# Four gates of the second branch made inside the delta rule of the last layer, and kept in the free half of the merge's sum buffer

## The chip, the cores and the metric

The kernel runs on one core of a Trainium2 chip. A core has five engines that run apart and meet through semaphores: TensorE (PE, matmuls into eight banks of PSUM; PEld is its weight load), VectorE (DVE), ScalarE (ACT), GpSimd (POOL) and SyncE (SP), which here only issues weight transfers. The metric is device time in microseconds of one launch. Everything is float32.

## The reference, cut to what matters

Two layers; each token stream has 256 context and 256 latent tokens (512 columns in all), and the model width is 1024.

```
px = in_projection(rmsnorm(x) * (1 + scale) + shift, w_in)
oa = bidirectional chunked gated linear attention        (branch 0, GLA)
ob = bidirectional chunked gated delta rule, conv'd q/k/v (branch 1, GDN)
oc = multi-head latent attention                          (branch 2, MLA)
y_i = head_norm(o_i) * silu(z_i)
ys  = y_i @ w_branch[i]                # per branch, 1024 x 1024
gates = sigmoid(px['merge_gate'])      # 3 branches x 1024 channels
x  = x + gate_x * (sum_i gates_i * ys_i) @ w_out
```

The second layer updates only the latent stream, so its merge works on 256 columns (LC to T) of each buffer, and the first 256 columns are free there.

## The kernel before, in words

**A list of items sets every engine's order.** `schedule()` writes one list of items, such as `("gate", l, br, e)`: layer `l`, branch `br`, block `e` of 128 output channels. Each engine's program walks that one list, so what is moved in it is moved on all engines at once. `weave` mixes several lists evenly by their load; `settle` then shifts some kinds by a fixed number of places. `pieces` cuts a long matmul item in four: a gate, or a `ys` product, is four pieces of two matmuls with 256 columns each, and the trace holds every such float32 matmul as two records. Banks and the four slots of the weight ring (`ring`, 1 MB a transfer) are dealt out in the order of this list.

**A gate.** PE makes the logits of 128 channels (8 matmuls). ACT takes absolute value, exp and ln(1+x) into one of two buffers `E1`, DVE a minimum and a subtraction (`("v", "gate", ...)`), and ACT's last exp gives the sigmoid. Normally that last exp belongs to the item `ys`; then DVE multiplies it by the product of `ys` and adds it into `MT`, the merge's sum buffer.

**Kept gates.** Six gates of branch 2 in the last layer are made early: `kept_gates` puts them into the delta rule, and an item `gx` writes their last exp into the context half of `yT`, where DVE's `ys` reads them.

**The delta rule of the last layer** (`gdn`) has four rounds `g`, two heads each. `head` prepares a round (`d1`, `d2`, `dd`, `dt`); `sol` solves the small triangular systems on POOL, with transfers before and after; `invert` (`dv` first, then `dx`, `dya`, `dyb`, `dx6`, `dy6`) puts the inverses together on PE, DVE and ACT; the scan (`st`, `su`, `sk`, `sq`, `sa`) follows. While POOL solves round g+1, PE projects q, k and v (`dqkv`) and scans round g. The list `fill` is spread over the rounds in shares 1, 1, 1, 2: first the kept gates, then the merge of branch 0 (8 gates and 8 `ys`).

**Latent attention** (`mla`) follows: low-rank projections (`mkv`, `mq`), the projections up (`muk`, `muq`, `mkT`, `mqT`), then scores, softmax and output (`ms`, `mp`, `mo`) in four rounds. Its first part is woven with the gate path of branch 1: `z` (matmul), `("v","z")` (DVE), `z2` (ACT exp, then three DVE operations, L1872, L1874, L1879) and `yT` (PE transposes, L1087, and a DVE copy, L1890). The rest is woven with the merge of branch 1, `m`. Its first `lead` items stand ahead of `rest`, mixed with the last transposes.

The lines that the prediction names: L1084 and L1087 the matmuls and the transposes, L1437 to L1439 ACT's three operations of a gate or a `z`, L1617 ACT's last exp, L1854 DVE's step on a `z`, L2104 the four DVE copies of `dv`, L2055 DVE's end of `dn`.

Of the kernel before, what the change touches and what calls it, by code (L numbers as in the profile page):

```python
# [9 lines left out]
ACT = mybir.ActivationFunctionType  # L10
# [7 lines left out]
DEPTH = 2  # L18
LC = LX = 256
T = LC + LX  # L20
# [100 lines left out]
    return NB // 2 - 1 - n if n < NB // 2 else 3 * NB // 2 - 1 - n  # L121


def keeps(it):

    return it[0] in ("gate", "ys") and it[1] == DEPTH - 1 and it[2] == 2 and it[3] < 6


def ahead(it):
# [24 lines left out]
def pieces(it):  # L154

    return [("pc",) + it + (i,) for i in range(NPIECE[it[0]] - 1)] + [it]
# [16 lines left out]
def schedule():  # L173
# [18 lines left out]
    def yts(l, br):  # L192
        return [("yT", l, br, tt, 1) for tt in tiles(l)]

    def kept_gates(l):

        out = []
        for e in range(6):
            out += pieces(("gate", l, 2, e)) + [("v", "gate", l, 2, e), ("gx", l, 2, e)]
        return out  # L200

    def merge(l, br):
        if keeps(("gate", l, br, 0)):
            out = [i for e in range(6, 8) for i in pieces(("gate", l, br, e)) + [("v", "gate", l, br, e)]]
            return out + [i for e in range(8) for i in pieces(("ys", l, br, e))]
        out = []
        for e in range(9):
            if e < 8:
                out += pieces(("gate", l, br, e))
            p = pieces(("ys", l, br, e - 1)) if e else []  # L210
            out += p[:2] + ([("v", "gate", l, br, e)] if e < 8 else []) + p[2:]
        return out

    def mods(todo):
# [144 lines left out]
    for l in range(DEPTH):  # L359
        s += [("nx", l)] * (l > 0) + [("nh", l)]  # L360
        s += gla(l)
        s += [("rstd", l, 0)]
        fill = merge(l, 0)
        if keeps(("gate", l, 2, 0)):
            fill = kept_gates(l) + fill
        s += gdn(l, zs(l, 0) + yts(l, 0), fill)
        s += [("rstd", l, 1)]
        first, rest = mla(l)
        lead = len(pieces(("gate", l, 1, 0))) + 1
        m = merge(l, 1)  # L370
        z = zs(l, 1)
        s += z[:5] + weave(first, z[5:] + weave(yts(l, 1), m[:lead]))
        s += weave(rest, m[lead:])
        m = merge(l, 2)
        lead = 5 * (8 - 6) if keeps(("gate", l, 2, 0)) else lead
        s += zs(l, 2) + weave(yts(l, 2), m[:lead]) + m[lead:]
        sums = pieces(("norm", l + 1)) if l < DEPTH - 1 else []
        for e in range(8):
            s += [("out", l, e)] + sums[e - 2:e - 1] * (e >= 2)
        if sums:  # L380
            s += sums[6:7] + [("mod", l + 1, 4)] + sums[7:] + [("modT", l + 1, 4), ("mod", l + 1, 5), ("modT", l + 1, 5)]
# [74 lines left out]
def hybrid_block(nc, x, c, ctx_in, c_ctx, norm_w, ada_w, ada_b, w_in, gla_gate_w2, gla_gate_b, gla_norm_w,  # L456
# [20 lines left out]
    for now, it in enumerate(plan):  # L477
        it = it[1:-1] if it[0] == "pc" else it
# [31 lines left out]
    with ExitStack() as stack:  # L510
# [5 lines left out]
        MT = sb("MT", [P, KT, T])  # L516
        yT = sb("yT", [P, KT, T])
# [15 lines left out]
        E1 = sb("E1", [P, 2, 512])  # L533
# [394 lines left out]
        zg_index = {i: n for n, i in enumerate(zg)}  # L928
# [503 lines left out]
        def _(act):  # L1432
# [43 lines left out]
            for it in plan:  # L1476
                k, l = it[0], it[1]
                if k == "nh":
                    act.wait_ge(*done(("modT", l, 5 if l else 3), "dve"))
                    act.wait_ge(s_scw, l + 1)  # L1480
                    for kk in range(KT):
# [3 lines left out]
                        for s in range(2):  # L1485
                            sel = 1 - s
                            ins = nc.scalar.activation(seg(hT[:, kk, :], s), seg(hT[:, kk, :], s), ACT.Identity,
                                                       bias=MOD[:, l, kk, sel:sel + 1], scale=SCW[:, kk, sel:sel + 1])
# [10 lines left out]
                if k == "xin":  # L1499
                    _, tt, h = it  # L1500
                    ins = nc.scalar.activation(yT[:, 4 * h:4 * h + 4, tt * P:(tt + 1) * P],
                                               ps[:, :].rearrange("p (j n) -> p j n", j=4), ACT.Copy)
                elif k == "xout":
                    _, tt, h = it
                    ins = nc.scalar.activation(O[:, tt, h * 512:(h + 1) * 512], ps[:, :], ACT.Copy)  # L1505
                elif k == "par":
# [4 lines left out]
                    ins = nc.scalar.activation(SCt[:, 0, :], PAR[:, l, PR_C:PR_C + 16], ACT.Exp, scale=-1.0) if l == 0 else \  # L1511
                        nc.scalar.activation(SCt[:, 1, 0:1], EPSC[:, :], ACT.Copy)
                elif k == "norm":
# [11 lines left out]
                    ins = rsqrt(RS[:, :], ps[:, :], D)  # L1525
                elif k == "lr":
                    ins = nc.scalar.activation(LRT[0:LROW, :], ps[0:LROW, :], ACT.Copy)
                elif k == "gqk":
                    _, l, g, j = it
                    a0 = q0 if j < 2 else 0  # L1530
                    ins = nc.scalar.activation(QK[:, g, j, a0:T], ps[:, a0:T], ACT.Copy)
                elif k == "gv":
                    _, l, g, tt = it
                    ins = nc.scalar.activation(V[:, g, tt, :], ps[:, :], ACT.Copy)
                elif k == "ga":
                    p = prev_kind(it)
                    if p:
                        act.wait_ge(*done(p, "dve"))
                    p = plan_prev(it, ("go",))
# [3 lines left out]
                    ins = log1p_exp(LT1, ps[:, :])  # L1543
                elif k == "gb":
                    p = prev_kind(it)
# [4 lines left out]
                    ins = nc.scalar.activation(EI, ps[:, :], ACT.Exp, scale=-1.0 / 16)  # L1550
                elif k == "ge":
                    p = prev_kind(it)
# [4 lines left out]
                    ins = nc.scalar.activation(AER, ps[:, :], ACT.Exp, scale=1.0 / 16)  # L1557
                elif k == "gw":
                    _, l, h, r, n = it
# [4 lines left out]
                    ins = nc.scalar.activation(HQ[:, r, n, :], HS[:, r, :], ACT.Copy, scale=AMID[:, r, at:at + 1])  # L1564
                elif k == "go":
                    _, l, h, tt = it
                    act.wait_ge(*done(plan_prev(it, ("go", "ga")), "act"))
                    if plan_prev(it, ("go", "ga"))[0] == "ga":
                        act.wait_ge(*done(plan_prev(it, ("ga",)), "dve"))
                    ins = nc.scalar.activation(LT1[:, 0:ADV], ps[:, 0:ADV], ACT.Square,  # L1570
                                               accum_out=SSQ[:, 0, tt, h:h + 1])
                elif k == "osq":
                    _, l, g, p = it
# [7 lines left out]
                    for i in range(4):  # L1581
                        tt, h = 2 * p + i // 2, 2 * g + i % 2
                        ins = nc.scalar.activation(RS[:, i * P:(i + 1) * P], O[:, tt, h * P:(h + 1) * P], ACT.Square,
                                                   accum_out=SSQ[:, 1, tt, h:h + 1])
                elif k == "rstd":
                    _, l, br = it
# [8 lines left out]
                    ins = rsqrt(SSQ[:, br, t0:TT, 0:nh], SSQ[:, br, t0:TT, 0:nh], hd)  # L1595
                elif k in ("z", "gate"):
                    n = zg_index[it]
                    if n >= 2:
                        p = zg[n - 2]
# [5 lines left out]
                    ins = log1p_exp(E1[:, n % 2, a0:512], ps[:, a0:512])  # L1605
                elif k == "gx":
                    gi = ("gate",) + it[1:]
                    act.wait_ge(*done(gi, "dve"))
                    act.wait_ge(s_spill, 16 * (l + 1))
                    act.wait_ge(s_scaled, KT * (l + 1))  # L1610
                    ins = nc.scalar.activation(yT[:, it[3], 0:LC], E1[:, zg_index[gi] % 2, LC:T], ACT.Exp)
                elif k in ("z2", "ys"):

                    zi = ("z" if k == "z2" else "gate",) + it[1:]
# [1 line left out]
                    e = E1[:, zg_index[zi] % 2, (q0 if k == "ys" else 0):512]  # L1616
                    ins = nc.scalar.activation(e, e, ACT.Exp)  # L1617
                elif k == "dg":
# [14 lines left out]
                    ins = nc.scalar.activation(ERV[:, :, :], ERV[:, :, :], ACT.Exp)  # L1633
                elif k == "dqkv":
                    act.wait_ge(s_zero, 4 * l + 3)
                    pj = dq_index[it] % 2
                    p = prev_kind(it, 2)
                    if p:
                        act.wait_ge(*done(("cv",) + p[1:] + (CONV - 1,), "dve"))
                    a0 = 1 if (it[3] < 2 and l == DEPTH - 1) else 0  # L1640
                    ins = nc.scalar.activation(PAD[:, 2 * pj + a0:2 * pj + 2, 2:258],  # L1641
                                               ps[:, a0 * LC:T].rearrange("p (s n) -> p s n", n=LC), ACT.Copy)
                elif k == "dsilu":
                    act.wait_ge(*done(("cv",) + it[1:] + (CONV - 1,), "dve"))
                    p = prev_kind(it)
# [4 lines left out]
                    ins = log1p_exp(CE[:, a0:T], CA[:, pj, a0:T])  # L1650
# [130 lines left out]
        def _(dve):  # L1781
            entered = set()
            V_ = nc.vector
            for it in plan:
# [113 lines left out]
                elif k == "ys":  # L1898
# [2 lines left out]
                    e = E1[:, zg_index[gi] % 2, q0:512]  # L1901
                    if keeps(it):
                        dve.wait_ge(*done(("gx",) + it[1:], "act"))
                        e = yT[:, e8, 0:LC]
                    else:
                        dve.wait_ge(*done(it, "act"))
                    m = MT[:, e8, q0:T]
# [380 lines left out]
```

## Time and profile before

| | us |
|---|---|
| median of 3 runs | 2272.14 (2269.09 to 2276.57) |
| the profiled execution | 2264.7 |
| its span | 2262.9 |
| mean granted TensorE clock | 0.979 |
| PE busy | 2144.7 (95%) |
| DVE, ACT, POOL busy | 929.3, 845.4, 363.9 |

The second layer's delta rule lies between about 1573 and 1940 us of the span, its latent attention between about 1941 and 2169. "busy" of PE counts modelled ends of pipelined matmuls; the true price of a matmul is read from the distance of its records' starts. The granted clock is given as a share of 2.4 GHz; it is either 1 or 0.5 at any time.

### The profile page before, as it was taken

What the parts mean: (1) busy time and instruction counts of PE and PEld (TensorE: products, weight loads), DVE (VectorE), ACT (ScalarE), POOL (GpSimd) and SP (SyncE); (2) the same over time, 40 slices, a digit from 0 to 9 for tenths busy, and PEclk for the clock granted to TensorE, in tenths of its full rate; (3) what the DMA queues carried; (4) which work ended last, traced back from release to release, by engine and by line L of the source; (5) the groups of instructions that cost most, each with busy time, mean ns of one, the idle gap of its engine ahead of it and who ended that gap; (6) DMA issues with size and microseconds to landing.
All of it is one profiled execution on the core that took longest, in us unless ns stands there. A gap on an engine that the chain in (4) does not pass through costs nothing. (4 is left out here: it accounts for less than half of the span.)

```text
span 2262.9 us, 31475 instructions
## 1 busy us (share of the span) xinstructions
PE 2144.7 (95%) x10970; PEld 1464.3 (65%) x10970; DVE 929.3 (41%) x2271; ACT 845.4 (37%) x2205; POOL 363.9 (16%) x591
## 2 busy tenths in 40 slices
PE   6999899999989999999999999999989978999998
PEld 3667576655555786555674446777576657877687
DVE  2023374757563325433331120236566653343321
ACT  2123263536443224444331112246455443244420
POOL 1000007071542000000000010000734752000000
PEclk8999999999999999999999999999999999999999
DMA  8224412211212022111222333121322222332333
GB/s 287 70 75 142 141 41 63 87 50 53 84 29 66 29 65 87 58 42 44 75 75 74 112 116 113 59 76 40 119 76 69 65 71 69 100 104 74 120 123 120
DMA packets 191420, 190.16 MB, mean 84 GB/s; under 512 B 28559, under 2 KB 185955, under 8 KB 190755
## 3 DMA queue, kind: packets, MB, share of 16 engines
q1 hardware_dynamic: 186048, 171.08, 23.9%
q0 software_dynamic: 3648, 16.72, 2.3%
q8 instruction: 93, 1.52, 0.3%
q10 hardware_dynamic: 1571, 0.34, 0.1%
q14 instruction: 60, 0.49, 0.1%
HBM read 178.62 MB, written 9.50 MB: 83 GB/s over the span
## 5 line engine op out<-in xcount | busy, mean ns | idle before, releaser
L1084 PE MATMUL bank<-hT,ring 128*128 128x512 f32 (+2 forms) x1856 | 718.8, 535 | 3.0 <-DVE hT L1845 1.5
L1084 PEld LDWEIGHTS bank<-hT,ring 128*128 128x128 f32 (+1 forms) x1856 | 332.6, 190 | 257.5 <-issue 240.0
L1084 PE MATMUL bank<-ring,hT 128*128 128x256 f32 (+2 forms) x2112 | 454.2, 370 | 11.6 <-DMA ring<-in_w_in_dram 11.6
L1084 PE MATMUL bank<-WORK 128*128 128x128 f32 (+6 forms) x3056 | 392.9, 287 | 42.0 <-DVE O L2104 17.7
L1084 PEld LDWEIGHTS bank<-ring,hT 128*128 128x128 f32 x2112 | 383.4, 192 | 75.2 <-issue 28.4
L1084 PEld LDWEIGHTS bank<-WORK 128*128 128x128 f32 (+4 forms) x3056 | 322.0, 171 | 145.9 <-issue 123.8
L1084 PE MATMUL bank<-yT,ring 128*128 128x512 f32 (+1 forms) x768 | 272.0, 492 | 0.0
L1084 PEld LDWEIGHTS bank<-yT,ring 128*128 128x128 f32 x768 | 140.4, 192 | 84.5 <-issue 76.0
L1048 POOL TENSOR_TENSOR WORK<-WORK 64x31 f32<-64x31 f32 (+15 forms) x248 | 152.0, 613 | 19.4
L2031 DVE SCALAR_TENSOR_TENSOR WORK<-WORK,CW 128x512 f32<-128x512 f32 (+1 forms) x192 | 147.1, 766 | 2.3
L1046 POOL TENSOR_TENSOR WORK<-WORK 64x31 f32<-64x31 f32 (+15 forms) x248 | 142.3, 574 | 19.5
L1437 ACT ACTIVATE E<-bank 128x512 f32<-128x512 f32 (+1 forms) x84 | 44.9, 535 | 253.5 <-PE bank L1084 253.3
L1072 POOL DMA_DIRECT2D yT<-xs x2 | 1.1, 536 | 808.0 <-DVE MT L1915 808.0
L1084 PE MATMUL bank<-ring,WORK 128*128 128x384 f32 (+1 forms) x272 | 108.4, 536 | 0.0
L1449 ACT ACTIVATE WORK<-bank 128x128 f32<-128x128 f32 (+3 forms) x182 | 47.2, 271 | 133.0 <-PE bank L1084 133.0
L1084 PE MATMUL bank<-MT,ring 128*128 128x512 f32 (+1 forms) x256 | 83.8, 486 | 2.7 <-DVE MT L1915 2.7
L1087 PEld LDWEIGHTS bank<-K,WORK 128*128 128x128 f32 (+1 forms) x506 | 64.9, 145 | 31.5 <-issue 23.8
L1087 PE MATMUL bank<-K,WORK 128*128 128x128 f32 (+1 forms) x506 | 82.9, 282 | 0.0
L1084 PEld LDWEIGHTS bank<-ring,WORK 128*128 128x128 f32 x272 | 50.3, 190 | 37.9 <-issue 22.0
L1084 PEld LDWEIGHTS bank<-MT,ring 128*128 128x128 f32 x256 | 48.5, 190 | 37.2 <-issue 30.1
L1933 DVE SCALAR_TENSOR_TENSOR WORK<-bank,WORK 128x512 f32<-128x512 f32 x16 | 11.1, 692 | 139.2 <-ACT WORK L1439 139.2
L1641 ACT ACTIVATE WORK<-bank 128x512 f32<-128x512 f32 (+1 forms) x48 | 26.8, 559 | 98.1 <-PE bank L1084 98.1
(205 smaller groups left out, 2085.1 us busy)
## 6 DMA issues: line engine op xcount, KB each, us to landing
ring<-in_w_in_dram SPq DMA_DIRECT2D x92, 1024.0 KB, 5.2
ring<-in_ada_w_dram SPq DMA_DIRECT2D x24, 1024.0 KB, 6.0
ring<-in_w_branch_dram SPq DMA_DIRECT2D x24, 1024.0 KB, 5.1
ring<-in_w_out_dram SPq DMA_DIRECT2D x8, 1024.0 KB, 5.0
ring<-in_mla_q_up_dram SPq DMA_DIRECT2D x8, 576.0 KB, 4.6
xs<-yT POOLq DMA_DIRECT2D x2, 2048.0 KB, 10.6
ring<-in_mla_kv_up_dram SPq DMA_DIRECT2D x8, 512.0 KB, 3.7
yT<-xs POOLq DMA_DIRECT2D x2, 2048.0 KB, 9.1
```

Source lines behind the costliest of these rows:

```text
L1046: link(pool, "pool", pool.tensor_tensor(t, a[:, j + 1:BASE, j:j + 1].broadcast_to([q, m, w]), y[:, j:j + 1, 0:w].broadcast_to([q, m, w]), ...
L1048: ins = pool.tensor_tensor(y[:, j + 1:BASE, 0:w], y[:, j + 1:BASE, 0:w], t, ALU.subtract)
L1072: pool.dma_start(yT[:, :, :], xs[l]).then_inc(s_back, 16)
L1084: return nc.tensor.matmul(o, a, b, start=start, stop=stop, skip_group_check=True)
L1087: return nc.tensor.transpose(o, a, ident)
L1437: link(act, "act", nc.scalar.activation(dst, src, ACT.Abs))
L1449: ins = nc.scalar.activation(MT2[:, c0:c0 + w], ps[:, c0:c0 + w], ACT.Square, accum_out=mS[:, at + i:at + i + 1])
L1641: ins = nc.scalar.activation(PAD[:, 2 * pj + a0:2 * pj + 2, 2:258], ps[:, a0 * LC:T].rearrange("p (s n) -> p s n", n=LC), ACT.Copy)
L1933: ins = V_.scalar_tensor_tensor(LA[:, tt, :], ps[:, :], 0.0, LT1, ALU.min, ALU.subtract)
L2031: ins = V_.scalar_tensor_tensor(acc, src, wv, acc, ALU.mult, ALU.add)
```

## The change

`KEPT` now holds how many gates of each branch are kept: none of branch 0, four of branch 1, six (as before) of branch 2. The four new ones are made in the delta rule behind the six, and are written into the context half of `MT`. The merge of branch 1 loses their pieces and the DVE step; and the number of items that lead it goes from five (one gate) to none.

```diff
+KEPT = (0, 4, 6)
+
+
 def keeps(it):
 
-    return it[0] in ("gate", "ys") and it[1] == DEPTH - 1 and it[2] == 2 and it[3] < 6
+    return it[0] in ("gate", "ys") and it[1] == DEPTH - 1 and it[3] < KEPT[it[2]]
...
         for e in range(9):
             if e < 8:
-                out += pieces(("gate", l, br, e))
+                out += [] if keeps(("gate", l, br, e)) else pieces(("gate", l, br, e))
             p = pieces(("ys", l, br, e - 1)) if e else []
-            out += p[:2] + ([("v", "gate", l, br, e)] if e < 8 else []) + p[2:]
+            out += p[:2] + ([("v", "gate", l, br, e)] if e < 8 and not keeps(("gate", l, br, e)) else []) + p[2:]
...
         if keeps(("gate", l, 2, 0)):
-            fill = kept_gates(l) + fill
+            fill = kept_gates(l, 2) + kept_gates(l, 1) + fill
         s += gdn(l, zs(l, 0) + yts(l, 0), fill)
         s += [("rstd", l, 1)]
         first, rest = mla(l)
-        lead = len(pieces(("gate", l, 1, 0))) + 1
+        lead = 0 if keeps(("gate", l, 1, 0)) else len(pieces(("gate", l, 1, 0))) + 1
         m = merge(l, 1)
         z = zs(l, 1)
         s += z[:5] + weave(first, z[5:] + weave(yts(l, 1), m[:lead]))
         s += weave(rest, m[lead:])
...
-                    ins = nc.scalar.activation(yT[:, it[3], 0:LC], E1[:, zg_index[gi] % 2, LC:T], ACT.Exp)
+                    ins = nc.scalar.activation((yT if it[2] == 2 else MT)[:, it[3], 0:LC], E1[:, zg_index[gi] % 2, LC:T], ACT.Exp)
...
-                        e = yT[:, e8, 0:LC]
+                        e = (yT if br == 2 else MT)[:, e8, 0:LC]
```

TensorE, the scan of the last round of the delta rule, from the first `st` on. `WORK x4` is a step of the scan, `hT,ring` are gate pieces and `yT,ring` pieces of `ys` of branch 0 (x2 is one piece). Before:

```order
L1084 MATMUL bank2<-WORK 128x128 x4
L1084 MATMUL bank5<-hT,ring 128x256 x2
L1084 MATMUL bank3<-WORK 128x128 x4
L1084 MATMUL bank5<-hT,ring 128x256 x2
L1084 MATMUL bank0<-WORK 128x128 x4
L1084 MATMUL bank5<-hT,ring 128x256 x2
L1084 MATMUL bank1<-yT,ring 128x256 x2
L1084 MATMUL bank7<-WORK 128x128 x4
L1084 MATMUL bank1<-yT,ring 128x256 x2
L1084 MATMUL bank6<-WORK 128x128 x4
```

And now (all lines of the program stand three further down):

```order
L1087 MATMUL bank4<-WORK 128x128 x4
L1087 MATMUL bank3<-yT,ring 128x256 x2
L1087 MATMUL bank2<-WORK 128x128 x4
L1087 MATMUL bank3<-yT,ring 128x256 x4
L1087 MATMUL bank7<-WORK 128x128 x4
L1087 MATMUL bank0<-hT,ring 128x256 x4
L1087 MATMUL bank6<-WORK 128x128 x4
L1087 MATMUL bank0<-hT,ring 128x256 x2
L1087 MATMUL bank5<-WORK 128x128 x4
L1087 MATMUL bank0<-hT,ring 128x256 x2
```

Between the same steps of the scan stand one or two pieces where there was one.

TensorE, where latent attention goes from its first part to the scores, from the second `muq` on. `ring,WORK` are `muq` and `muk`, `K,O x4` is a `yT`, `K,WORK` a transpose of keys (x2) or queries (x3), `hT,ring` a gate piece. Before:

```order
L1084 MATMUL bank5<-ring,WORK 128x384 x3
L1084 MATMUL bank3<-ring,WORK 128x512 x2
L1084 MATMUL bank0<-hT,ring 128x256 x2
L1087 MATMUL bank7<-K,WORK 128x128 x2
L1087 MATMUL bank4<-K,O 128x128 x4
L1087 MATMUL bank6<-K,WORK 128x128 x2
L1084 MATMUL bank2<-ring,WORK 128x512 x2
L1084 MATMUL bank0<-hT,ring 128x256 x2
L1087 MATMUL bank5<-K,WORK 128x128 x2
L1084 MATMUL bank0<-hT,ring 128x256 x2
L1087 MATMUL bank3<-K,WORK 128x128 x3
L1087 MATMUL bank1<-K,O 128x128 x4
```

And now:

```order
L1087 MATMUL bank3<-ring,WORK 128x384 x3
L1087 MATMUL bank1<-ring,WORK 128x512 x2
L1090 MATMUL bank7<-K,O 128x128 x4
L1090 MATMUL bank4<-K,WORK 128x128 x2
L1087 MATMUL bank2<-ring,WORK 128x512 x2
L1090 MATMUL bank6<-K,WORK 128x128 x2
L1090 MATMUL bank3<-K,WORK 128x128 x2
L1090 MATMUL bank1<-K,O 128x128 x4
L1090 MATMUL bank7<-K,WORK 128x128 x3
L1090 MATMUL bank4<-K,O 128x128 x4
L1090 MATMUL bank2<-K,WORK 128x128 x2
L1090 MATMUL bank0<-K,O 128x128 x4
```

The gate pieces are gone from here, and all four `yT` now stand behind the last `z`, close to each other (one stood ahead of the first `muq` before).

VectorE at the same place: L1854 (L1857 now) is the step on the last `z`, L1872 to L1879 (L1875 to L1882) a `z2`, L1890 (L1893) the copy of a `yT`. Before:

```order
L1854 SCALAR_TENSOR_TENSOR E1<-bank1,E1 128x512
L1872 TENSOR_TENSOR E1<-E1,bank4 128x512
L1874 TENSOR_TENSOR O<-O,SSQ 128x512
L1879 TENSOR_TENSOR O<-O,E1 128x512
L2216 TENSOR_TENSOR WORK<-bank6,WORK 128x256
L1890 TENSOR_TENSOR yT<-bank2,NW4 128x4x128
```

And now, from the last `muk` (L2219) on:

```order
L2219 TENSOR_TENSOR WORK<-bank2,WORK 128x256
L1875 TENSOR_TENSOR E1<-E1,bank0 128x512
L1877 TENSOR_TENSOR O<-O,SSQ 128x512
L1882 TENSOR_TENSOR O<-O,E1 128x512
L1857 SCALAR_TENSOR_TENSOR E1<-bank5,E1 128x512
L1893 TENSOR_TENSOR yT<-bank1,NW4 128x4x128
L2239 TENSOR_SCALAR WORK<-bank7,QKW 128x2x128
L1875 TENSOR_TENSOR E1<-E1,bank5 128x512
L1877 TENSOR_TENSOR O<-O,SSQ 128x512
L1882 TENSOR_TENSOR O<-O,E1 128x512
```

Both last `z2` now stand behind the last `muk`, close together; before, thirteen other instructions stood between the two, and the first was ahead of the last `muk`.

## Rows read from the trace of the kernel before

**Rows 1.** The page: the kernel's engines, busy time and share.

```profile
PE 2144.7 (95%) x10970; PEld 1464.3 (65%) x10970; DVE 929.3 (41%) x2271; ACT 845.4 (37%) x2205; POOL 363.9 (16%) x591
```

**Rows 2.** Busy time by stretch, last layer; first the stretch and its length.

```profile
core 0: us, PE busy (x) PEld busy (x) DVE busy (x) ACT busy (x) POOL busy (x), PEclk, DMA share, GB/s
1584.60:1651.00 66.40, 55.92 (x200) 35.51 (x198) 37.52 (x61) 25.22 (x48) 45.40 (x69) 0.96 0.41 125
1673.20:1736.00 62.80, 61.56 (x279) 41.64 (x277) 41.69 (x86) 31.23 (x70) 43.14 (x69) 1.00 0.32 95
1736.00:1756.70 20.70, 18.20 (x302) 16.25 (x301) 15.86 (x45) 16.01 (x43) 0.00 (x0) 0.92 0.09 21
1756.70:1816.00 59.30, 57.19 (x253) 38.37 (x252) 39.95 (x78) 28.04 (x63) 43.33 (x69) 1.00 0.24 69
1816.00:1831.30 15.30, 11.66 (x80) 10.33 (x79) 11.26 (x32) 9.82 (x26) 0.00 (x0) 1.00 0.52 149
1831.30:1889.20 57.90, 40.82 (x432) 34.65 (x432) 25.62 (x67) 19.94 (x52) 40.72 (x69) 0.90 0.18 53
1889.20:1940.00 50.80, 50.17 (x476) 43.51 (x477) 18.61 (x53) 16.71 (x45) 0.08 (x1) 0.94 0.26 84
2024.50:2169.00 144.50, 144.50 (x673) 103.13 (x672) 50.98 (x168) 66.19 (x252) 0.00 (x0) 1.00 0.26 85
```

**Rows 3.** Busy time by stretch, three with the half clock.

```profile
1649.40:1656.10 6.70, 4.37 (x82) 3.79 (x84) 5.95 (x19) 2.30 (x5) 0.00 (x0) 0.50 0.01 2
1833.70:1843.80 10.10, 5.33 (x44) 4.24 (x44) 2.35 (x6) 4.08 (x11) 6.61 (x13) 0.50 0.07 27
1888.30:1895.10 6.80, 5.84 (x84) 4.51 (x85) 2.21 (x8) 5.78 (x16) 0.00 (x0) 0.50 0.01 2
```

**Rows 4.** The chain that ended last, around 1885 us: start, length, what.

```profile
1883.85 4.25 DMA WORK<-XD
...
1889.26 3.13 PE bank L1084 x62
```

**Rows 5.** The same chain, behind latent attention.

```profile
2190.81 3.46 PE bank L1084 x16
...
2225.12 27.88 PE bank L1084 x128
```

**Rows 6.** TensorE in order of time, in brackets the idle time before.

```profile
1651.73 0.55 PE L1084 MATMUL bank<-WORK 128*128 128x128 f32 x1 [5.74 <-DVE WORK L2055]
...
1889.26 0.23 PE L1084 MATMUL bank<-WORK 32*32 32x32 f32 x1 [6.22 <-DVE O L2104]
```

**Rows 7.** Groups of TensorE by shape, 2024.5 to 2169 us: the gates' pieces.

```profile
L1084 PE MATMUL bank<-hT,ring 128*128 128x256 f32 x112 | 28.9, 382 | 0.0
```

**Rows 8.** VectorE in order of time, around the first of the last two `z2`.

```profile
2013.69 0.68 DVE L1854 SCALAR_TENSOR_TENSOR E<-bank,E 128x512 f32<-128x512 f32 x1
2014.29 0.68 DVE L1872 TENSOR_TENSOR E<-E,bank 128x512 f32<-128x512 f32 x1
...
2015.60 0.69 DVE L1879 TENSOR_TENSOR O<-O,E 128x512 f32<-128x512 f32 x1
...
2020.88 0.69 DVE L1879 TENSOR_TENSOR O<-O,E 128x512 f32<-128x512 f32 x1
2021.49 0.68 DVE L1890 TENSOR_TENSOR yT<-bank,NW 128x512 f32<-128x512 f32 x1
2022.09 0.41 DVE L2216 TENSOR_TENSOR WORK<-bank,WORK 128x256 f32<-128x256 f32 x1
```

**Rows 9.** ScalarE: the last exp of a `z2`, and its first and last operation of a `muk`.

```profile
2018.40 0.61 ACT L1617 ACTIVATE E<-E 128x512 f32<-128x512 f32 x1
...
2020.34 0.38 ACT L1742 ACTIVATE WORK<-bank 128x256 f32<-128x256 f32 x1 [0.78 <-PE bank L1084]
...
2021.60 0.20 ACT L1459 ACTIVATE WORK<-WORK 128x2 f32<-128x2 f32 x1
```

**Rows 10.** TensorE from the first to the last transposes of branch 1.

```profile
2006.78 0.60 PE L1087 MATMUL bank<-K,O 128*128 128x128 f32 x4
...
2022.41 0.60 PE L1087 MATMUL bank<-K,O 128*128 128x128 f32 x4
2022.85 0.38 PE L1087 MATMUL bank<-K,WORK 128*128 128x128 f32 x2
```

More of the change, by code:

```diff
@@ L193, in yts, with kept_gates @@
         return [("yT", l, br, tt, 1) for tt in tiles(l)]
-    def kept_gates(l):
+    def kept_gates(l, br):
         out = []
-        for e in range(6):
-            out += pieces(("gate", l, 2, e)) + [("v", "gate", l, 2, e), ("gx", l, 2, e)]
+        for e in range(KEPT[br]):
+            out += pieces(("gate", l, br, e)) + [("v", "gate", l, br, e), ("gx", l, br, e)]
         return out
     def merge(l, br):
-        if keeps(("gate", l, br, 0)):
+        if br == 2 and keeps(("gate", l, br, 0)):
             out = [i for e in range(6, 8) for i in pieces(("gate", l, br, e)) + [("v", "gate", l, br, e)]]
@@ L374, in schedule @@
         m = merge(l, 2)
-        lead = 5 * (8 - 6) if keeps(("gate", l, 2, 0)) else lead
+        lead = 5 * (8 - 6) if keeps(("gate", l, 2, 0)) else len(pieces(("gate", l, 2, 0))) + 1
         s += zs(l, 2) + weave(yts(l, 2), m[:lead]) + m[lead:]
```

## The prediction

> **What bounds the kernel now.** First the page: PE is busy 95% of the span and no other engine over 41% [rows 1]. So what counts is PE's time, and the question is only where PE still waits. I read that from the busy time by stretch [rows 2], in which the last layer's delta rule is cut where its rounds hand over. Three kinds of stretch are seen.
>
> PE-bound ones: 1673.2 to 1736.0 and 1756.7 to 1816.0, the POOL solves of rounds 1 and 2 (counted from 0). PE is busy 61.56 of 62.80 and 57.19 of 59.30 us [rows 2], although POOL works beside it. Latent attention from 2024.5 to 2169 is busy for all of its 144.50 us [rows 2].
>
> One that waits for POOL: 1831.3 to 1889.2, the solve of round 3. PE is busy only 40.82 of 57.90 us, so it idles 17.1 us [rows 2]. The chain runs through POOL and its transfer, and PE starts only behind it [rows 4], after a last wait of 6.22 us for DVE's `dv` [rows 6].
>
> Short ones bound by DVE, ACT and PE in turn: 1736.0 to 1756.7 and 1816.0 to 1831.3. Then 1889.2 to 1940, round 3's inversion and scan, with PE busy for 50.17 of 50.80 us [rows 2].
>
> **The price of a piece.** Eight matmuls with 256 columns are 16 records; 3.46 us of the chain hold 16 of them [rows 5]. A piece is two matmuls, so 0.865 us. The end of the chain confirms it: 64 matmuls in 27.88 us are 0.871 us for two [rows 5]. Four gates are sixteen pieces, 13.8 us of PE, which leave latent attention and enter the delta rule. (The mean of 382 ns a record [rows 7] can't be used for this: the records overlap.)
>
> **Where the pieces arrive.** I counted gate and `ys` pieces of the last layer in the list before and after, between the marks of the stretches:
> - up to the start of round 1's solve: 4 and 4;
> - from there to round 1's `dx`: 12 and 15, so 3 more, 2.6 us, where PE is the bound;
> - in round 1's inversion: 3 and 3;
> - from the start of round 2's solve to that of round 3: 15 and 18, 3 more, 2.6 us, PE-bound but for its last 15 us, which get no more than they had;
> - from the start of round 3's solve to its `dx`: 22 and 24, 2 more, 1.7 us, in the stretch with 17.1 us of idle PE. They cost nothing as long as POOL is late; without this cover they would cost 1.7 us;
> - from round 3's `dx` to the end of the delta rule: 32 and 40, 8 more, 6.9 us.
>
> The sum is 16. Fourteen stand where PE has no room: 12.1 us. Three of the last eight stand in round 3's inversion, a chain over DVE and ACT as well, and one `dqkv` piece moves into round 1's inversion, where PE waits; I take 1.1 us off: **+11.0 us**, between +8 (all that is woven into inversions and scan stalls hidden, for which 0.6 us of idle PE behind 1889.2 [rows 2] speaks poorly) and +13.8.
>
> The other work of the four gates is small: three ACT operations and a `gx`, one DVE operation. It leaves attention and enters the delta rule, where ACT is busy 31.23 of 62.80 us and DVE 41.69 [rows 2]; both are below PE, and the new steps stand beside steps of the same kind. 0, at most +2 us, if some of them delays a piece of the scan. The two weight transfers move along; each has tens of us of other work between the release of its slot and its first use.
>
> **What latent attention gives back.** Twelve of the sixteen pieces stand between the scores' start and the end: 10.4 us. It is busy throughout, with no idle time before it [rows 2, 7], so I count them in full, less 1.0 us for a few short distances (keys' projection to transposition, scores to softmax) which lose a piece: **-9.4 us**.
>
> The other four were `lead`, 3.5 us among the last transposes. Here I expect the change to lose. Before, PE had 15.6 us of work between the first and the last `yT` [rows 10], and the last one came without a wait: DVE's last `z2` had ended at 2020.88 + 0.69 = 2021.57 and PE began at 2022.41 [rows 8, 10]. In the new order both last `z2` stand behind the last `muk` on DVE. From the end of that `muk` on PE the chain is: ACT's part, 2020.34 to 2021.80, 1.46 us; its exp 0.61 [rows 9]; a `z2`, from 2014.29 to 2015.60 + 0.69, 2.0 us; the step on the last `z` 0.6; the copy of a `yT` 0.6; the queries' scaling 0.4; the other `z2` 2.0 [rows 8]. Sum 7.6 us. PE has in that time two transposes of keys, one of queries, two `yT` and one more of keys; a `yT` of four transposes takes 0.44 us [rows 10], the whole 1.9 us. So it waits some 5.7 us, in two waits around the third `yT`. Against the 3.5 us of pieces that are gone, this place ends 2 us later than before: **+2.0 us**, between -3.5 (no wait) and +4.
>
> Then the clock. Behind waits of 5.74 and 6.22 us [rows 6] PE's granted clock is 0.50 for 6.7 and 6.8 us [rows 3], the 1.2 GHz level. I expect the same here, for 3.4 to 6.8 us, and PE at half speed loses half of it: **+2.4 us**, from 0 to +3.4. The half clock around 1838 and 1888 [rows 3] lies in or behind POOL's stretch as before.
>
> **The sum.** 11.0 - 9.4 + 2.0 + 2.4 = +6.0 us on the profiled execution's 2264.7, so 2270.7. Its time is 7.4 below the median of the runs shown, 2272.1; on that footing the forecast is **2278 us**. About 0.3%, 6.8 us, is what a measurement of this kernel can tell from no change, so +6.0 is just inside.
>
> **The rivals.**
>
> Faster: the delta rule has idle PE, and the pieces fill it. For it: 17.1 us idle in one stretch alone and 3.6 more in 1816 to 1831 [rows 2]. Were all sixteen covered and no new wait made, the time would fall by 9.4 + 3.5 = 12.9 us; with half of them covered and the wait at the entry, nothing would be gained. Against it: the shares of `fill` put two of sixteen pieces into that stretch. Its mechanism would be that POOL paces rounds 1 and 2 too, so that their six pieces are free (-5.2), that half of the last eight go into hidden stalls (-3.4), and that the entry to attention ends where it did (0 for 2.0 and 2.4): 2.4 - 9.4 = -7.0 us, 2265.
>
> Neutral: the counts are right but the entry to attention does not wait, as DVE and ACT have less to do there than I take. Then 11.0 - 9.4 - 3.5 = -1.9 us, 2270. For it: before, the same steps ended 0.8 us early [rows 8, 10].
>
> Slower by more: attention is not bound by PE's matmuls, and gives back only a part. It decides from the point where PE, with fewer pieces, has to wait for the softmax (ACT is busy 66.19 of 144.50 us there [rows 2]). With half of the 9.4 us lost: +10.7, 2283. Against it: PE is busy without a gap [rows 2], and 0.865 us apiece is the distance of starts and not a modelled end [rows 5].
> The Trainium skill bears on this one, in "Perfetto Trace Analysis", section "Identifying the Most-Contended Engine": a busy share of matmuls is a poor measure of PE's headroom, and the share of the weight loads is to be read. That share is 103.13 of 144.50 us here, 71%. By this rule a third of the stretch would be headroom, and an estimate by it lets the twelve pieces give back some two thirds, 6.3 us, which makes +9.1 in all.
>
> That the change doesn't do what it says is excluded by the order: the gates stand in the delta rule, and attention has 48 gate and `ys` pieces left of 64.
>
> **How the numbers follow.** Forecast 0.58, neutral 0.16, faster 0.09, slower by more 0.17. The forecast's own uncertainty is about 4 us each way, so of its 0.58 I put 0.33 within 0.3% and 0.25 above it. The neutral case lies within, the slower one above; of the faster one 0.07 is under -0.3%. Together faster 0.07, same 0.51, slower 0.42. The range of 8 in 10 leaves out a tenth on each side: from 2266 (the faster case's edge) to 2286 (the slower one with POOL's cover gone as well).
>
> **What would show it.** Right: the starts of round 2's and round 3's solves 2.6 and 5.2 us later; PE's idle time between round 3's solve and its `dx` smaller by about 2 us; round 3's `dx` to the end of the delta rule longer by about 7; a wait of PE before an L1090 transpose for DVE's L1882, 5 to 6 us, where there was none, and the half clock behind it; from the scores' start to the end of attention about 9 us less. Wrong: solves that start at most 1 us later (faster), no such wait (neutral), or new waits of PE in the scores and softmax (slower).

## The result, and the profile after

| | before | after |
|---|---|---|
| median, us | 2271.07 (4 runs, 2269.09 to 2276.57) | 2287.28 (4 runs, 2284.50 to 2290.88) |
| profiled execution | 2264.7 | 2288.93 |
| its span | 2262.9 | 2287.1 |
| mean granted TensorE clock | 0.979 | 0.972 |

The ratio is 1.0068, 95% interval [1.0044, 1.0092]: 15.4 us slower, where +6.0 was forecast. The time lies 1.3 us above the range.

The two profiled executions must not be subtracted whole. Up to the last layer's first `d1`, where both kernels issue the same work, they already differ by 9.4 us (1563.6 and 1573.0). From that `d1` to the end of the last output's product it is 689.4 us before and 704.3 after, unrounded **+14.8 us**, close to the timed +15.4. So every difference below is one of lengths, each taken between two events of one execution.

The page's engines, answering to [rows 1]. PE's busy time is no less than before, in a longer span.

```profile
PE 2155.1 (94%) x10970; PEld 1470.1 (64%) x10970; DVE 930.5 (41%) x2271; ACT 845.3 (37%) x2205; POOL 361.4 (16%) x591
```

Busy time by stretch of after, answering to [rows 2, 3]: start and end, length, then busy time (records) of PE, PEld, DVE, ACT, POOL, the granted clock, the share of the DMA engines and their GB/s.

```profile
1594.00:1660.40 66.40, 55.70 (x200) 35.41 (x198) 37.36 (x61) 25.22 (x48) 45.35 (x69) 0.96 0.42 125
1682.60:1745.40 62.80, 61.09 (x276) 41.53 (x276) 42.53 (x85) 30.58 (x68) 42.74 (x69) 1.00 0.32 93
1767.00:1829.60 62.60, 61.14 (x276) 42.11 (x275) 40.00 (x81) 31.19 (x69) 42.49 (x69) 1.00 0.29 86
1829.60:1844.90 15.30, 11.59 (x69) 10.25 (x67) 10.99 (x30) 8.09 (x23) 0.00 (x0) 0.89 0.34 100
1844.90:1904.90 60.00, 42.82 (x444) 36.56 (x444) 24.81 (x66) 22.21 (x58) 40.90 (x69) 0.88 0.26 78
1904.90:1960.00 55.10, 54.99 (x501) 48.54 (x502) 18.98 (x54) 17.68 (x44) 0.00 (x0) 0.95 0.25 78
1897.20:1910.90 13.70, 5.91 (x88) 4.72 (x89) 2.62 (x9) 5.86 (x16) 1.20 (x1) 0.50 0.18 55
2047.40:2054.20 6.80, 5.56 (x13) 2.95 (x15) 2.35 (x4) 0.00 (x0) 0.00 (x0) 0.50 0.00 0
2020.00:2055.10 35.10, 29.55 (x113) 18.68 (x112) 17.25 (x43) 16.75 (x68) 0.00 (x0) 0.90 0.38 124
2055.10:2192.90 137.80, 132.40 (x615) 93.02 (x616) 49.31 (x162) 60.15 (x236) 0.00 (x0) 1.00 0.25 78
```

The row to 1960.00 ends with the last `sa`. Before, the last `sa` ends at 1938.5, so the row to 1940.00 of [rows 2] is 1.5 us longer than that stretch, and the lengths to compare are 49.3 and 55.1 us.

The last two rows are the entry to latent attention and the rest of it. The mark between them is the end of the first pair of scores: PE issues the scores of two heads together, and the last matmuls of both stand in the second one's item, so that neither can be used earlier. The entry runs from the end of the last `mq` to this mark, the rest from the mark to the end of the last `mo`; below they are called "ahead of" and "behind the first scores". The same two stretches of before:

```profile
1999.40:2027.20 27.80, 27.80 (x121) 18.76 (x120) 17.23 (x44) 16.38 (x69) 0.00 (x0) 1.00 0.56 174
2027.20:2168.70 141.50, 141.50 (x664) 102.13 (x664) 50.26 (x165) 65.17 (x248) 0.00 (x0) 1.00 0.27 87
```

Here is the point that the forecast missed. Behind the first scores PE is busy for 141.50 - 132.40 = 9.1 us less, about what was expected (9.4). But the stretch is only 3.7 us shorter: 5.4 us have turned into idle time. PE in order of time, with the idle time before each group in brackets; the first row answers to the last of [rows 6]:

```profile
1904.99 0.23 PE L1087 MATMUL bank<-WORK 32*32 32x32 f32 x1 [11.77 <-DVE O L2107]
...
2045.12 0.63 PE L1090 MATMUL bank<-K,O 128*128 128x128 f32 x4 [2.58 <-DVE O L1882]
...
2048.64 1.09 PE L1090 MATMUL bank<-K,O 128*128 128x128 f32 x4 [2.67 <-DVE O L1882]
...
2057.88 2.58 PE L1087 MATMUL bank<-WORK 128*128 128x512 f32 x6 [1.77 <-DVE WORK L2239]
...
2089.26 0.41 PE L1090 MATMUL bank<-K,WORK 128*128 128x128 f32 x2 [0.75 <-DVE WORK L2219]
...
2096.49 1.10 PE L1087 MATMUL bank<-WORK 128*128 128x512 f32 x2 [1.79 <-DVE WORK L2239]
```

The two waits for L1882 are the forecast ones. Those for L2239, the scaling of queries (`mqT`), were not foreseen. What stands before it on ACT and DVE, after:

```profile
2055.13 0.69 DVE L2249 TENSOR_REDUCE WORK<-bank 128x1 f32<-128x512 f32 x1 [4.68 <-PE bank L1087]
2055.86 0.15 DVE L2250 TENSOR_SCALAR WORK<-WORK 128x1 f32<-128x1 f32 x1
2056.09 0.69 ACT L1769 ACTIVATE WORK<-bank,WORK 128x512 f32<-128x512 f32 x1 [9.58 <-PE bank L1087]
2056.68 0.19 ACT L1769 ACTIVATION_READ_ACCUMULATOR WORK<-bank,WORK 128x1 f32 x1
2056.77 0.27 ACT L1760 ACTIVATE WORK<-bank 128x128 f32<-128x128 f32 x1
2057.15 0.48 DVE L2239 TENSOR_SCALAR WORK<-bank,QKW 128x256 f32<-128x256 f32 x1 [1.14 <-ACT WORK L1760]
```

The first score's maximum (L2249, L2250) and its exp (L1769) stand ahead of the copy (L1760) and the scaling (L2239) of the round's last queries, each on its engine. The maximum itself had waited 4.68 us for the end of the first pair. So the scores of the last 128 queries wait for the softmax of the first score. Before, the scaling came first and the maximum second, and PE did not wait:

```profile
2025.68 0.48 DVE L2236 TENSOR_SCALAR WORK<-bank,QKW 128x256 f32<-128x256 f32 x1 [1.60 <-ACT WORK L1757]
...
2027.28 0.69 DVE L2246 TENSOR_REDUCE WORK<-bank 128x1 f32<-128x512 f32 x1 [1.11 <-PE bank L1084]
```

The reason is in `settle`: it moves each `ms` two places earlier, whatever stands there. Before, in the list ahead of this shift, one item of the merge lay between the last `mqT` of each round and its first `ms` (DVE's step of gate 0 in round 0, a piece of gate 3, 5 or 7 in the others). With gates 0 to 3 gone nothing lies there in rounds 0 and 1, and the `ms` passes the `mqT`; in rounds 2 and 3 a piece of a `ys` product still lies there, and there is no such wait.

### The profile page after: what moved, and what is told of

Read it like the earlier page. It is cut to its first block and busy times, and to the rows that moved or that the text cites. A ratio compares the mean times of both kernels' runs of the same rounds, so it can differ in the third digit from the quotient of the medians.

```text
span 2287.1 us, 31483 instructions
## 1 busy us (share of the span) xinstructions
PE 2155.1 (94%) x10970; PEld 1470.1 (64%) x10970; DVE 930.5 (41%) x2271; ACT 845.3 (37%) x2205; POOL 361.4 (16%) x591
## 5 line engine op out<-in xcount | busy, mean ns | idle before, releaser
L1087 PE MATMUL bank<-WORK 128*128 128x128 f32 (+6 forms) x3056 | 400.1, 290 | 50.7 <-DVE O L2107 24.2
L1087 PEld LDWEIGHTS bank<-WORK 128*128 128x128 f32 (+4 forms) x3056 | 326.6, 174 | 156.5 <-issue 133.6
L1936 DVE SCALAR_TENSOR_TENSOR WORK<-bank,WORK 128x512 f32<-128x512 f32 x16 | 11.1, 692 | 140.1 <-ACT WORK L1442 140.1
## 6 DMA issues: line engine op xcount, KB each, us to landing
xs<-yT POOLq DMA_DIRECT2D x2, 2048.0 KB, 11.2
```

Of the source, the lines that this page charges most:

```text
L1087: return nc.tensor.matmul(o, a, b, start=start, stop=stop, skip_group_check=True)
L1936: ins = V_.scalar_tensor_tensor(LA[:, tt, :], ps[:, :], 0.0, LT1, ALU.min, ALU.subtract)
```

## The experiments

The letters A to D are those of the expectations; B and D mean something else in each run and are defined there. A is the account above: a piece costs 0.865 us where PE has no room and nothing where PE waits for POOL, and waits come from fixed shifts in a list that has become shorter. C is the prediction's rival "slower by more": attention isn't bound by PE. Each change in microseconds is the ratio times 2271. "The region" is again from the last layer's first `d1` to the last output's product, minus the 689.4 us of before. It comes from one execution of each kernel, and the time from several. In the edits, `...` marks what is left out.

**e1: the attention half alone.** The four gates are made nowhere (`ys` reads what the sum buffer holds), and the merge of branch 1 is as in after.

```diff
-            fill = kept_gates(l, 2) + kept_gates(l, 1) + fill
+            fill = kept_gates(l, 2) + fill
...
```

(The lines left out let DVE's `ys` go on without waiting for a gate.)

> The attention half of the change alone: the four gates of branch 1 are left out altogether (neither made in the delta rule nor in attention; its sums use what stands in the buffer), so 13.8 us of TensorE are gone from attention and nothing is added. Theory A (the trace of after: from the end of the delta rule to the end of the kernel it is 2.7 us longer than before, for all its missing pieces; the two waits at the entry, 2.6 and 2.7 us, and two of 1.8 us in which a score waits for the queries' scaling, take back the gain): before +1 to +4 us. Theory B (the attention gives back what the prediction said, -9.4 +2.0 +2.4 = -5, and the rest of the loss is made in the delta rule): before -5 us or less.

Measured: 2274.02 (12 runs), ratio 1.0012 [1.0003, 1.0022], +2.7 us; region +1.7. Taking 13.8 us of matmuls away makes the kernel no faster. The waits are those of after, in PE's order of time:

```profile
2028.51 0.63 PE L1090 MATMUL bank<-K,O 128*128 128x128 f32 x4 [2.64 <-DVE O L1882]
2032.02 1.09 PE L1090 MATMUL bank<-K,O 128*128 128x128 f32 x4 [2.67 <-DVE O L1882]
2041.04 3.01 PE L1087 MATMUL bank<-WORK 128*128 128x512 f32 x8 [1.76 <-DVE WORK L2240]
```

**e2: the delta-rule half alone.** Four extra gates are made in the delta rule and read by nobody; attention keeps its own.

```diff
-        for e in range(KEPT[br]):
+        for e in range(6) if br == 2 else range(8, 12):
...
```

(The lines left out keep gates 0 to 3 in attention and say where the extra ones are written.)

> The delta rule's half alone: four gates more are made in the delta rule of the last layer (of other channels, written to the free half of the sum buffer and not read), and attention keeps all of its gates and its order. Two more weight transfers in all. Theory A (fourteen of sixteen pieces stand where TensorE has no room; the trace of after is 12.1 us longer there): before +11 to +13 us. Theory B (the delta rule loses more than TensorE's price, by ScalarE and the weight ring): before +17 us or more. If the idle time of the solves took the pieces up, it would be +3 us or less.

Measured: 2283.38, ratio 1.0060 [1.0045, 1.0075], +13.6 us, 0.6 above what was expected; region +11.2. The two halves add: 2.7 + 13.6 = 16.3, against 15.4 of the whole. Attention is untouched and PE is full in it:

```profile
1905.90:1961.30 55.40, 55.22 (x501) 48.77 (x502) 19.05 (x55) 17.70 (x44) 0.00 (x0) 0.94 0.25 77
2049.10:2190.70 141.60, 141.60 (x663) 102.18 (x664) 50.30 (x165) 65.26 (x248) 0.00 (x0) 1.00 0.27 87
```

**e3: after, without two shifts.** In the last layer `ms` and `z2` are not shifted any more (the 1 in a key is the layer).

```diff
-AHEAD = {... 'mod': -1, 'gatt': -6, ...}
+AHEAD = {... 'mod': -1, ('ms', 1, 0): 0, ('z2', 1, 0): 0, 'gatt': -6, ...}
```

> After, with two of the fixed shifts in the list set to 0 in the last layer: z2 (four places later before) and ms (two places earlier before). With that the first of the last two z2 stands ahead of the last muk, and the last mqT ahead of the first ms, as in the kernel before. Theory A: the score's waits for the scaling (1.8 us at the entry and 1.8 in the second round, each with some us of half clock or knock-on) go, and the entry's waits shrink: after -5 to -10 us. Theory B: within 2 us of after.

Measured: 2277.84, ratio 1.0032 [1.0020, 1.0045], +7.3 us, so 8 us of after's loss are gone by moving places alone; region +7.8. No wait for L2239 is left. The two at the entry are smaller, 3.7 us instead of 5.3 together, and one of them is now for the keys' projection (L2219):

```profile
2040.75 0.41 PE L1090 MATMUL bank<-K,WORK 128*128 128x128 f32 x2 [2.21 <-DVE WORK L2219]
2044.99 1.09 PE L1090 MATMUL bank<-K,O 128*128 128x128 f32 x4 [1.52 <-DVE O L1882]
```

**e4: after, the gates put under the last solve.** The shares of `fill` in the last layer are counts written out, so that the added pieces fall into the stretch in which POOL solves round 3. (Two more numbers, for where a round's share is cut in two, follow from it.)

```diff
-            upto = round(len(fill) * sum(share[:g + 1]) / sum(share))
+            upto = (22, 43, 89, 132)[g] if l == DEPTH - 1 else round(len(fill) * sum(share[:g + 1]) / sum(share))
...
```

> After, with the fill divided otherwise: the stretch of the last solve gets 40 pieces (22 before, 24 after), the rounds ahead of it and the round behind it as many as before or two fewer. That is 15.6 us of TensorE in a stretch with 17.1 us of idle time. Theory A (the place of the pieces is what costs in the delta rule): the delta rule is 0 to +3 us against before, attention as in after: after -9 to -12 us, so before +3 to +6 us. If the solve stretch is really paced by dependences of the scan and not by GpSimd, the pieces lengthen it: within 4 us of after.

Measured: 2273.04, ratio 1.0012 [1.0000, 1.0024], +2.7 us: 12 to 13 us of after's loss are gone; region +1.5. The last solve and the scan behind it:

```profile
1833.70:1892.80 59.10, 52.62 (x496) 46.43 (x496) 27.15 (x70) 25.40 (x66) 40.83 (x69) 0.96 0.30 88
1892.80:1941.70 48.90, 48.31 (x469) 42.14 (x470) 17.93 (x51) 16.14 (x40) 0.00 (x0) 0.95 0.29 87
```

PE has 496 records there, 64 more than before [rows 2], which are sixteen pieces or 13.8 us; the stretch is 59.10 us long where it was 57.90. What is left of the loss is attention's.

One comparison is missing here. The kernel before had the same 17.1 us of idle PE, and its `fill` could have been divided in this way too, without any new gate. No run tries that, so e4, e8, e9 and e10 show what the place of the pieces is worth, and not that keeping four more gates gains anything over a kernel before with its own pieces placed as well.

**e5: the last four gates instead of the first four.** Gates 4 to 7 of branch 1 are kept, so that the pieces around the entry and in rounds 0 and 1 stay.

```diff
-        for e in range(KEPT[br]):
+        for e in range(4, 8) if br == 1 else range(KEPT[br]):
...
```

(`keeps` names the same four.)

> After, but the four kept gates of branch 1 are its last (4 to 7) and not its first. So the leading gate and its place among the last transposes stay, mqT stands ahead of ms in all rounds, and the last two z2 stand ahead of the last muk; the delta rule gets the same sixteen pieces. Theory A (attention loses its gain at its entry and by the crossed order, not by being short of pieces): the entry as before, attention gives back most of 13.8 us; with the delta rule's +12: before -3 to +2 us. Theory C (attention isn't bound by TensorE, it gives back little wherever the pieces are taken): before +8 us or more.

Measured: 2274.36, ratio 1.0011 [0.9998, 1.0025], +2.5 us; region -4.9. The timed value is 0.5 us above what was expected, and the profiled execution (2262.45) is the fastest of its 12 runs, so only the split is used here. (2.3 us of the region's -4.9 are round 0's solve, the same work in every kernel: POOL took 57.63 us for it in this execution and 59.89 before.) The entry takes 27.80 us, to the hundredth as before, and the rest 131.90 where it had 141.50.

```profile
2006.80:2034.60 27.80, 27.80 (x121) 18.77 (x120) 17.23 (x44) 16.38 (x69) 0.00 (x0) 1.00 0.51 156
2034.60:2166.50 131.90, 129.17 (x602) 90.24 (x601) 48.55 (x162) 59.17 (x232) 0.00 (x0) 1.00 0.26 81
```

**e6 and e7: each shift of e3 alone.**

```diff
-AHEAD = {... 'mod': -1, 'gatt': -6, ...}
+AHEAD = {... 'mod': -1, ('ms', 1, 0): 0, 'gatt': -6, ...}
```

```diff
-AHEAD = {... 'mod': -1, 'gatt': -6, ...}
+AHEAD = {... 'mod': -1, ('z2', 1, 0): 0, 'gatt': -6, ...}
```

> After, with the shift of ms alone set to 0 in the last layer, so that the last mqT of each round stands ahead of the round's first ms. Theory A: the two waits of 1.8 us for the scaling and what hangs on them go, the two entry waits of 2.6 us stay: after -4 to -6 us. If the waits only move to the entry: within 2 us of after.

> After, with the shift of z2 alone set to 0 in the last layer: the first of the last two z2 stands ahead of the last muk on ScalarE and VectorE. The run with both shifts was 8 us faster than after and its entry still waited 2.2 and 1.5 us. Theory A: after -1 to -4 us, the rest of the 8 being the ms shift's.

Measured: e6 2284.39, ratio 1.0061 [1.0047, 1.0075]; e7 2281.20, ratio 1.0050 [1.0036, 1.0065]. Against after that is -1.6 and -4 us. By time e6 is a miss, as -4 to -6 was expected; but the interval of after's ratio alone is 5 us wide each way, so these times settle nothing between the two. By region it is +9.9 for e6 and +12.8 for e7, that is 4.9 and 2.0 less than after. The traces split this, with the marks as above:

| us | before | after | e6 (`ms`) | e7 (`z2`) | e3 (both) |
|---|---|---|---|---|---|
| last `mq` to first scores | 27.82 | 35.12 | 36.06 | 33.05 | 33.77 |
| first scores to last `mo` | 141.50 | 137.87 | 132.05 | 137.86 | 132.05 |

Without the shift of `ms` the stretch behind the first scores is 5.8 us shorter, whether `z2` is shifted or not. But 0.9 us of this is a `ys` piece that now stands ahead of the mark (610 records behind it instead of 614), so over entry and rest together the shift is worth 4.9 us (after against e6) and 5.1 us (e7 against e3). That of `z2` is worth some 2 us at the entry. In e6 the entry has become 0.9 us longer: the piece, and the half clock, which lasts for 10.2 us instead of 6.8, against 0.6 us less of idle time.

**e8: e5 and e4 together.** The last four gates, under the last solve.

> The last four gates of branch 1 kept, and the fill divided so that the stretch of the last solve takes all the additional pieces (40 instead of 22). Theory A: the delta rule costs nothing (as the run with the gates in the last solve showed) and attention gives back 13.8 us but for an us or two: before -10 to -13 us, ratio 0.995. Theory C: before -2 us at best.

Measured: 2264.17 (10 runs), ratio 0.9973 [0.9962, 0.9983]: 6.1 us **faster** than before; region -9.5. The direction was right and the size was not: attention gave back 9.7 us for 13.8 us of pieces. Of the rest the trace shows waits of 2.7 us, over short distances again: from the keys' projection (L2219) to their transposes, and from the copy of the transposed keys (L1754) to a score. PE in order of time:

```profile
2065.24 0.74 PE L1090 MATMUL bank<-K,WORK 128*128 128x128 f32 x5 [0.75 <-DVE WORK L2219]
2066.61 1.10 PE L1087 MATMUL bank<-WORK 128*128 128x512 f32 x2 [0.63 <-ACT WORK L1754]
2101.38 1.10 PE L1087 MATMUL bank<-WORK 128*128 128x512 f32 x2 [0.24 <-ACT WORK L1754]
2136.59 0.74 PE L1090 MATMUL bank<-K,WORK 128*128 128x128 f32 x5 [0.74 <-DVE WORK L2219]
2137.57 1.10 PE L1087 MATMUL bank<-WORK 128*128 128x512 f32 x2 [0.24 <-ACT WORK L1754]
```

**e9: the whole change with both mends**, e3's shifts and e4's shares.

> The whole change (gates 0 to 3 kept, as in the changed kernel) with both mends at once: the shares of fill of e4, and the two shifts of e3. Theory A (two independent places: pieces woven where PE is the bound, and fixed shifts at the entry to attention): the two effects add. The stretch that the change touches was 1.5 us longer than before in e4, and the two shifts took 7.0 us off it in e3; together -5.5 us against before, 2264 to 2268, some 6 us below e4. PE waits for the first L1882 only some 2 us and not at all for L2239. Rival D (the shifts only helped because the delta rule came late, or the shorter delta rule brings the ring's transfers late at the entry): no gain over e4, 2271 to 2275.

Measured: 2264.94 (7 runs), ratio 0.9970 [0.9955, 0.9984], 6.8 us faster than before; region -6.4. The same four gates as in the changed kernel, made in the same layer and kept in the same place, are 22 us faster than after by the order alone. The two mends add (12.7 and 8.1 us of after's loss, 22.2 together), which rival D denied. Entry and rest:

```profile
2002.10:2034.90 32.80, 29.49 (x118) 19.52 (x117) 17.42 (x44) 17.02 (x69) 0.00 (x0) 0.95 0.41 132
2034.90:2166.90 132.00, 130.51 (x611) 92.42 (x612) 48.84 (x161) 59.80 (x235) 0.00 (x0) 1.00 0.26 81
```

The two waits at the entry are 2.22 us, for L2219, and 0.94 us, for L1882, where some 2 us for L1882 were expected; for L2239 there is none.

**e10: e8 with wider distances.** The first score two places later, the keys' projection three earlier.

```diff
-AHEAD = {... 'mod': -1, 'gatt': -6, ...}
+AHEAD = {... 'mod': -1, ('ms', 1, 0): 0, ('muk', 1, 0): -3, 'gatt': -6, ...}
```

> e8 (the last four gates kept, in the last solve) with two more numbers of the last layer changed: the first score two places later and the projection of the keys three places earlier. Theory A (the 4.2 us that attention failed to give back in e8 are short distances in the list, from the keys' projection to their transposes and from the queries' scaling to the first score): the PE waits of 0.75 us for L2219 go, the scores' start to the end of attention is 2 to 4 us shorter, 2260 to 2262. Rival C (ACT or the weight loads set the pace of attention once the pieces are gone): the waits go and the time stays at 2264 or above.

Measured: 2262.66 (6 runs), ratio 0.9951 [0.9933, 0.9969], 11.1 us faster than before and 0.7 above the expected 2260 to 2262; region -11.8. By time alone its interval still touches e8's; the regions put it 2.3 us ahead, 1.8 of them in attention. Entry and rest:

```profile
2007.10:2037.90 30.80, 29.16 (x126) 19.42 (x124) 17.58 (x45) 16.16 (x69) 0.00 (x0) 1.00 0.46 141
2037.90:2165.00 127.10, 126.78 (x597) 89.49 (x596) 48.06 (x160) 58.87 (x232) 0.00 (x0) 1.00 0.27 84
```

Behind the first scores only 0.32 us of 127.10 are idle, and the stretch is 14.4 us shorter than before's 141.50. Part of that has gone to the entry, which is 3.0 us longer: it holds one piece more, since the scores start two places later, and one wait for a `z2` came:

```profile
2032.23 0.63 PE L1090 MATMUL bank<-K,O 128*128 128x128 f32 x4 [1.45 <-DVE O L1882]
```

Net, 11.4 of the 13.8 us are back.

## Why the prediction was wrong, point by point

| term | predicted | in the traces |
|---|---|---|
| delta rule | +11.0 | +12.1 |
| attention behind the first scores | -9.4 | -3.6 |
| entry, the pieces against the waits, and the clock | +2.0 + 2.4 | +6.3 |
| sum | +6.0 | +14.8 |

The row of the delta rule runs to its last `sa`; that of the entry is +7.3 us from the last `mq` on and -1.0 ahead of it. Of the 8.8 us between forecast and trace, 5.8 are attention's.

**The failing step is "What latent attention gives back".** Its sentence on a busy stretch, "so I count them in full, less 1.0 us for a few short distances", took one number for two things. That PE had no idle time before says that PE was the bound; it doesn't say that anything would be ready earlier once PE has less to do. The work did go: 664 - 615 = 49 records, some twelve pieces, as counted. But 5.4 us came back as idle time, and some 3.6 were gained, not 9.4. e3, e6 and e9 show that most of it is one shift of two places: without it the stretch takes 132.05 us, 9.5 less than before. That this is the forecast's 9.4 is in part luck, for thirteen pieces are gone from the stretch there and not twelve: 11.2 us of work gave back 9.5, a loss of 1.8 us to short distances where 1.0 was allowed. The order of after was there to be read: `ms` ahead of `mqT` in rounds 0 and 1. I looked for such a crossing at the `z2`, found it, and did not look for it at the other kinds that `settle` shifts.

**The delta rule: right in its sum, less so by parts.** It was forecast at +11.0 and measured at +12.1 in the profile; e2's extra gates alone are timed at +13.6. By parts: up to round 3's solve +4.2, where +5.2 was expected (round 1's solve took its three pieces for 0.95 us instead of 2.6, round 2's stretch 3.3 for 2.6); round 3's `dx` to the last `sa` +5.8, where 6.9 - 1.1 was written. By the prediction's own sign, the starts of the solves on POOL, round 2's came only 0.5 us later instead of 2.6, and round 3's 5.2, as was said. So round 1 hid 1.7 us of its three pieces.

In the last solve PE is idle for 60.00 - 42.82 = 17.2 us, as before, and not 2 us less; instead the stretch became 2.15 us longer. 1.0 us of this lies ahead of POOL's first transfer, which began 2.40 us into the stretch before and 3.41 after, but 2.40 again in e3 and e5 with the same pieces. The other 1.1 us is POOL's own solve, 51.36 us before and 52.50 after; with the same shares it took 51.04 (e5) to 53.17 (e3), and 52.6 to 53.1 in e4, e8, e9 and e10 with sixteen pieces more. So it goes with the execution more than with the pieces, whose cover e4 shows; a small cost of theirs isn't excluded.

**The entry: right in kind, 1.9 us short.** The waits for L1882 are 2.58 + 2.67 us, with 0.30 ahead of them, so 5.55 where 5.7 was worked out. The half clock behind them is 6.8 us long, the upper end of the forecast. PE's own busy time rose by 29.55 - 27.80 = 1.75 us there although 3.5 us of pieces are gone, a difference of 5.2. The half clock accounts for 2.8 of it: it set in during the second wait, so PE was busy for 5.56 of its 6.80 us and lost half of that. Another 1.7 are one `z` piece, eight records (40 against 32), which stood ahead of the last `mq` and now stands behind it; I had not counted it, and it is missing in the stretch ahead, which is 1.0 shorter. The remaining 0.7 stays open. The prediction read the half clock of [rows 3] as lying behind the waits in its whole length; in the two that it names it had begun 2.3 and 1.0 us before their ends.

**The rivals.** "Faster" needed covers that were there only in part, 1.7 us in round 1; it falls with e2, whose added gates alone cost 13.6 us. "Neutral" needed an entry without waits, and it has 5.6 us of them. "Slower by more" came nearest, and not by its number alone, 2283: its sign, new waits of PE in the scores behind the softmax, came, and so did its size: it had half of the 9.4 us lost, and 5.8 were. What the runs deny is its reason, that attention isn't bound by PE's matmuls. In e3 most of the loss goes with the order, and in e10 nearly all of the removed work turns into time once the distances are wider.

The Trainium skill ("Perfetto Trace Analysis", section "Identifying the Most-Contended Engine") judges TensorE's headroom by MFU (the matmuls' arithmetic as a share of the peak) and by the share of the weight loads. That share was 102.13 of 141.50 us, 72%, before, and is 89.49 of 127.10, 70%, in e10, although the stretch became 14.4 us shorter with 67 records less, 14.5 us at 0.216 us each. So the estimate that the prediction drew from it, that a third of the removed work would give nothing back, fails here. How near the matmuls are to the chip's peak, which is what that section asks, no run here tests.

**The place was the other half of the question.** I had written that only two of the sixteen pieces fall into the stretch with 17.1 us of idle PE, and priced the rest in full. e4 shows that this was the largest choice of the change: the same pieces put there save 12 to 13 us against after.

## What to carry to other kernels

When work is taken out of an engine's full stretch, check every pair of producer and consumer whose distance the removed work made up, on each engine that runs the same list; a fixed shift of places is a distance in time only as long as what it shifts past stays. When work is moved, ask first which stretch idles: here the same four gates cost 15.4 us in one order, and in another the kernel was 6.8 us faster than before. And when the mend also moves old work, run the old kernel with that mend too; this was not done here.

## What the runs showed of the hardware

- The wait of 11.77 us of PE, to 1904.99, has the half clock from 1897.2 to 1910.9; the one of 6.22 us before, to 1889.26, from 1888.3 to 1895.1 [rows 3, 6]. The half clock set in during the wait, and behind it PE ran at half speed for 5.9 and 5.8 us. So the longer wait did not make PE work at half speed for longer.
- Two waits of 2.58 and 2.67 us, 3.5 us apart, had 6.8 us of it. In e9 waits of 2.22 and 0.94 us had 3.4 us of it, from 2025.6 to 2029.0, and in e10 a single wait of 1.45 us at the same place had none (clock 1.00 over the entry).
- The busy time of PE, whose ends are modelled, doesn't follow the work exactly. In after 49 records less are worth 10.6 us at 0.216, and busy fell by 9.1; in e10 it was 67 records, 14.5 us, and busy fell by 14.7. Why isn't shown.
- Work ahead of the change, the same in every kernel, ended between 1563.6 and 1575.7 us over the profiled executions. A difference of a few microseconds between two spans says nothing until it is taken from a mark behind that part. And even behind it POOL's first solve, again the same work, took 57.63 (e5) to 61.33 us (e3), so a single region is good to some 2 us at best.
